# The recurrence of the odd layer: 32x32 chunk inverses by row substitution on VectorE in place of batched 128x128 products

## Chip, cores and metric

The kernel runs on one core of a Trainium2 chip. The metric is the device time of one execution in microseconds, lower is better. All data is float32.

## What is computed

The reference is a transformer of one block followed by a two-layer block (an even layer, an expert feed-forward, an odd layer, an expert feed-forward), for 512 tokens and 256 context tokens of width 1024. The change touches one part of the odd layer, a gated linear recurrence (RWKV-7) with 8 heads of 64, in both directions, which first runs over the context and then, from the state this leaves, over the tokens:

```python
def wkv7_step(S, inp):
    r, w, k, v, a, b = inp
    sa = jnp.einsum('bhvk,bhk->bhv', S, a)
    S = S * w[:, :, None, :] + sa[..., None] * b[:, :, None, :] + v[..., None] * k[:, :, None, :]
    return S, jnp.einsum('bhvk,bhk->bhv', S, r)

def direction(inp, d, S0):
    r, v, kk, w, a, k_eff, _ = inp
    a_d, k_d = a[:, :, d], k_eff[:, :, d]
    S, y = wkv7_scan(S0, r, w[:, :, d], k_d, v, -kk, kk * a_d, reverse=(d == 1))
    return S, y + jnp.sum(r * k_d * rk, -1, keepdims=True) * v
```

Computed by chunks of 32 tokens, each chunk of each head needs the inverse of I - N, where N is the strictly triangular 32x32 matrix of the products of the chunk's a and b vectors.

## The kernel before, in words

Every engine executes one list of instructions in the order in which the program emits them, and waits at semaphores. A `Core` object holds the counters and the PSUM banks of one line of work. `settle` makes an engine wait until all that the line has counted so far is done. `products` and `products_together` emit, group by group, the matmuls into a bank and the instruction that empties it; both begin with a settle of the engines they use, so that within a line one call waits for the one before it. `weave` takes generators and emits one piece of each in turn, up to the next `yield`; that order is the order on every engine.

The odd layer (`odd_layer`, L3132) loads its constants (`rwkv_constants`, L2901, with the loads at L140), projects the inputs (`rwkv_inputs`), runs the recurrence (`rwkv`, L2937), and goes on with neighbourhood attention and the output. The recurrence begins after all input is there, and the next stage begins with a load of X that waits for its end (L3164).

In `rwkv`, each direction d is one line with four PSUM banks, and `weave` alternates between the two lines. A line (`rwkv_direction`, L2696) goes through six rounds, one for each tile of 128 tokens: first the two context tiles, then the four token tiles. In this text the first two rounds are context rounds, and the other four (the code's `latent`) are token rounds. One round does this, for 8 heads, each with 4 chunks of 32 that stand on the diagonal of a 128x128 matrix:

- preparation: the decay and the rate from two small products (L2720, L2722), sums in the chunk (L2740), exponentials on ScalarE (L2746 to L2748), and element-wise products on VectorE (L2756 to L2774), which yield a, b, k and r with the decays multiplied in;
- transposes of a, b and k on TensorE (L402), with the banks emptied by VectorE and ScalarE in turn;
- `grams` (L2674, products at L2682, masks at L2689): b by a, a by b, and k by a, each masked to the chunks; b by a falls into blocks of 16 (B) and the part below them (Lo);
- the product of the masked k by a with the values (L2785), emptied at L2789, and Q = B + I (L2792);
- eleven jobs of `batched` (L2649): eight products of 128x128 by 128x128 each (L2655), emptied by ScalarE (L314) or, with an addition, by VectorE (L2664). They square B and accumulate the inverse of I - B in Q, and then solve in three more products with Lo between them;
- in token rounds two more grams with r;
- for each chunk three small products of 32 rows (L2830, L2832, L2834), emptied at L2841, and in token rounds one more product (L2816, L2839);
- four steps of the state, one for each chunk: product (L2854), addition (L2861), multiplication with the decay (L2862);
- in token rounds the output: products at L2871, L2875, L2878 and L2883, then three instructions of VectorE (L2892 to L2895).

## Time and profile before

| | |
|---|---|
| median of 3 runs | 4760.57 us (4752.04 to 4763.97) |
| profiled execution, span from first to last instruction | 4764.7 us |
| the recurrence (from L2713 to L2894) | 3096.7 to 3801.5 us, 704.8 us, 15% of the span |
| TensorE (PE) busy, whole span | 3841.3 us, 81% |
| VectorE (DVE) busy, whole span | 1379.7 us, 29% |
| ScalarE (ACT) busy, whole span | 724.6 us, 15% |

Of the profiled execution the span is what is listed; it lies 4.1 us above the median of the runs. In the rows below a matmul of float32 counts as two instructions, so a group of "x768" is 384 products of the code. "busy" of a group is the time in which at least one of its instructions ran; PE and PEld (the load of the stationary operand) overlap. PEclk 1.00 is the clock of 2.4 GHz, 0.50 that of 1.2 GHz. "<-" names what ended an engine's idle time. Busy share says little about the worth of a change here, since the stages have different limits; the reader should look at the stretch of the recurrence alone.

### The profile page before, as it was taken

Reading aid. Unit: us, or ns where it says so; the run is one execution under the profiler, and the core shown is the slowest. Engines: PE = TensorE matmul, PEld = TensorE weight load, DVE = VectorE, ACT = ScalarE, POOL = GpSimd, SP = SyncE. Lnnn points to the kernel's source line nnn. Section 1 sums busy time; section 2 is a strip of 40 time slices with the busy share of each in tenths; the row PEclk is TensorE's granted clock in tenths of the full one; section 3 lists DMA queues with packets and bytes.
Section 4 is the critical chain, followed back from the end, with each engine's and each line's share of the span. In section 5 each row is a group of like instructions: output and inputs, shape, how many; then the busy total and the mean of one; then the engine's idle time right before and its main releaser. Section 6 shows DMA issues by size and latency. Waiting matters only on the chain. (4 is left out here: it accounts for less than half of the span.)

```text
span 4764.7 us, 55924 instructions
## 1 busy us (share of the span) xinstructions
PE 3841.3 (81%) x23612; PEld 2364.9 (50%) x23612; DVE 1379.7 (29%) x2585; ACT 724.6 (15%) x1366; POOL 114.7 (2%) x88
## 2 busy tenths in 40 slices
PE   7998788888977875894899976877888769947776
PEld 3666356555523543783333324577777725632222
DVE  2312222322321077543100002245544423320000
ACT  1112001001011023311100001122222122210000
POOL 0000000000000000000011110000000000000000
PEclk9988798888888987996899998977888889969999
DMA  3200132443441100003799982000000011069999
GB/s 115 71 18 1 44 111 73 137 133 98 147 174 60 36 21 0 27 19 139 287 395 397 394 292 88 22 1 1 2 2 2 28 66 50 11 232 402 404 402 361
DMA packets 238285, 626.76 MB, mean 132 GB/s; under 512 B 38212, under 2 KB 90132, under 8 KB 230998
## 3 DMA queue, kind: packets, MB, share of 16 engines
q1 hardware_dynamic: 227990, 600.11, 33.6%
q0 software_dynamic: 10048, 23.07, 2.1%
q8 instruction: 190, 3.11, 0.3%
q14 instruction: 57, 0.47, 0.0%
HBM read 588.40 MB, written 34.75 MB: 131 GB/s over the span
## 5 line engine op out<-in xcount | busy, mean ns | idle before, releaser
L379 PE MATMUL bank<-weights_l,hT_l 128*128 128x512 f32 (+2 forms) x1824 | 605.7, 493 | 26.8 <-DMA weights_l<-in_w_in 20.0
L379 PEld LDWEIGHTS bank<-weights_l,hT_l 128*128 128x128 f32 x1824 | 386.2, 216 | 241.5 <-issue 173.6
L375 PE MATMUL bank<-hT_l,weights_l 128*128 128x512 f32 (+1 forms) x928 | 329.8, 518 | 39.6 <-DMA weights_l<-in_w_in 25.1
L1730 PE MATMUL bank<-expert_weights_l,expert_tokensT_l 128*32 128x512 f32 x3072 | 338.3, 596 | 11.4 <-DMA expert_weights_l<-in_moe_w 9.8
L1930 PE MATMUL bank<-expert_weights_l,expert_tokensT_l 128*64 128x512 f32 x1024 | 243.5, 622 | 82.8 <-DMA expert_weights_l<-in_moe_w 81.8
L375 PEld LDWEIGHTS bank<-hT_l,weights_l 128*128 128x128 f32 x928 | 179.2, 194 | 188.9 <-issue 165.3
L1240 PE MATMUL bank<-hT_l,gate_weights_r 128*128 128x512 f32 x384 | 213.7, 708 | 24.0 <-DMA gate_weights_r<-in_w_in 24.0
L1730 PEld LDWEIGHTS bank<-expert_weights_l,expert_tokensT_l 128*32 128x32 f32 x3072 | 107.8, 110 | 227.9 <-issue 226.9
L1930 PEld LDWEIGHTS bank<-expert_weights_l,expert_tokensT_l 128*64 128x64 f32 x1024 | 80.0, 142 | 236.2 <-issue 177.4
L1765 PE MATMUL bank<-expert_weights_l,rows 128*32 128x512 f32 x1536 | 167.9, 592 | 0.9 <-ACT rows L1805 0.9
L1930 PE MATMUL bank<-expert_weights_l,hiddenT_l 128*64 128x512 f32 x512 | 119.9, 610 | 47.0 <-DMA expert_weights_l<-in_moe_w 47.0
L1240 PEld LDWEIGHTS bank<-hT_l,gate_weights_r 128*128 128x128 f32 x384 | 83.5, 228 | 123.3 <-issue 104.5
L379 PE MATMUL bank<-weights_l,mixedT_l 128*128 128x256 f32 (+1 forms) x512 | 138.3, 433 | 2.4 <-ACT mixedT_l L314 1.4
L1486 PE MATMUL bank<-identity,normed_l 128*128 128x128 f32 x224 | 37.8, 351 | 126.7 <-ACT normed_l L452 75.3
L379 PEld LDWEIGHTS bank<-weights_l,mixedT_l 128*128 128x128 f32 x512 | 97.1, 190 | 42.8 <-issue 32.9
L1815 DVE TENSOR_TENSOR rows<-rows,bank 128x512 f32<-128x512 f32 x16 | 11.0, 688 | 368.5 <-ACT rows L1797 368.5
L1178 DVE SCALAR_TENSOR_TENSOR state_l<-state_l,exp_cumulative_l,bank 128x128 f32<-128x128 f32 x224 | 62.8, 343 | 176.5 <-PE bank L1161 173.8
L2664 DVE TENSOR_TENSOR rows<-rows,bank 128x512 f32<-128x512 f32 x96 | 65.9, 688 | 151.9 <-PE bank L2655 146.9
L1765 PEld LDWEIGHTS bank<-expert_weights_l,rows 128*32 128x32 f32 x1536 | 53.5, 110 | 111.7 <-issue 110.6
L1993 DVE TENSOR_TENSOR hidden_l<-silu_l,bank 128x512 f32<-128x512 f32 x16 | 11.0, 687 | 322.8 <-PE bank L1930 322.8
L2655 PE MATMUL bank<-rows,powers_then_steps_l 128*128 128x128 f32 x768 | 103.3, 294 | 0.0
L1613 POOL DMA_INDIRECT expert_rows_l<-normed_rows,row_numbers_l x16 | 15.4, 960 | 3651.6 <-DVE row_numbers_l L1609 3647.3
(471 smaller groups left out, 5247.8 us busy)
## 6 DMA issues: line engine op xcount, KB each, us to landing
expert_weights_l<-in_moe_w SPq DMA_DIRECT2D x192, 2048.0 KB, 24.9
ada_weights_r<-in_ada_w SPq DMA_DIRECT2D x48, 1024.0 KB, 5.0
weights_l<-in_w_in SPq DMA_DIRECT2D x10, 2048.0 KB, 8.0
weights_l<-in_w_in SPq DMA_DIRECT2D x16, 1024.0 KB, 5.3
gate_weights_r<-in_w_in SPq DMA_DIRECT2D x12, 1024.0 KB, 6.4
weights_l<-in_od_w_in SPq DMA_DIRECT2D x7, 1024.0 KB, 5.4
gate<-gate_rows_r SPq DMA_DIRECT2D x24, 256.0 KB, 2.4
weights_l<-in_ev_w_in SPq DMA_DIRECT2D x3, 2048.0 KB, 10.6
```

What stands on the lines that cost most here:

```text
L375: ins = pe.matmul(bank[:n, :m], w_sb[:, k, s:s + n], xT[:, k, t:t + m], start=k == 0, stop=k == kt - 1)
L379: ins = pe.matmul(bank[:rows_of_tile(x), :n], x, w_sb[:, k, :n], start=k == 0, stop=k == kt - 1)
L1178: ins = dve.scalar_tensor_tensor(out=new[:, s], in0=old[:, s], scalar=cum[:, hh, c * CH + edge:c * CH + edge + 1], in1=kv_bank[i % 2][:, s ...
L1240: ins = pe.matmul(bank[:, :], w[:, k, s:s + P], hT[:, k, :], start=k == 0, stop=k == KT - 1)
L1486: ins = pe.transpose(bank[:, (t - a) * P:(t - a) * P + P], xn[:, t, k * P:k * P + P], ident[:, :])
L1613: pool.indirect_dma_start(out=rows[:, q, :], out_offset=None, in_=normed[w], in_offset=bass.IndirectOffsetOnAxis(ap=idx[:, q:q + 1], axis= ...
L1730: return pe.matmul(bank[q * STRIP:(q + 1) * STRIP, :], xs[:, k, e, g * STRIP:(g + 1) * STRIP], w[:, j, h * HALF:(h + 1) * HALF], start=k = ...
L1765: return pe.matmul(bank[q * STRIP:(q + 1) * STRIP, :], rows, w2[:, f % DEEP, m * HALF:(m + 1) * HALF], start=f == first, stop=f == last)
L1815: dve.tensor_tensor(hid, hid, w3_bank[:, :], ALU.mult)
L1930: ins = pe.matmul(bank[h * S:h * S + S, :], rows(k), ring[r][:, k % DEEP, h * HALF:(h + 1) * HALF], start=k == 0, stop=k == KT - 1)
L2655: ins = pe.matmul(bank[:, j * P:j * P + P], lhs[:, m, :], rhs[:, m, :], start=True, stop=True)
L2664: return e.tensor_tensor(dst[:, s, :], add[:, s, :], src, ALU.add)
```

## The change

The inverse of each 32x32 matrix is computed directly. The masked 128x128 products b by a and a by b become 32x32 products of the chunks alone (64 matrices of both directions). They are stored to DRAM and loaded again, so that each of 64 partitions holds one 32x32 matrix; VectorE then substitutes row by row, with two instructions for each of 30 rows, and the inverses go back through DRAM: for direction 0 into the diagonal blocks of Q, for direction 1 into a tile whose blocks VectorE transposes into Q. Ten of the eleven `batched` jobs, the masks 2 and 3, Lo, Am, A2 and the addition of I fall away.

The preparation of both directions becomes a third line, `ahead`, which works one round ahead of the two others; the substitution is cut into six pieces that are emitted between the pieces of the current round. The banks are dealt 3, 3 and 2 instead of 4 and 4. The tiles that preparation writes exist twice. The transposes and the product with the values are emptied by ScalarE. In the steps of the state, the products with b and k are accumulated in the same bank as the product with the state, so that one instruction of VectorE is left for each step; the output is accumulated in one bank along with the steps, and the bonus term is written to Y by the preparation. In `rwkv_constants` the four loads into `sums_in_chunk` go, the mask load becomes two smaller ones, and one small constant is added.

```diff
+    out["above_diagonal"] = np.tile(np.triu(np.ones((32, 32), f), 1), (4, 1))
-def rwkv_direction(core, d, C, U, kkT, vnat, ups, cols, consts, mats, Y):
+ROUNDS = (((4, 5, 0, 1, 2, 3), (5, 4, 3, 2, 1, 0)))
+def rwkv_prepare(core, rnd, C, U, kkT, ups, cols, consts, sides, Y):
+    products(core, 4, fill, take, lambda i: "v" if i < 2 else "s", ready=True)
+    core.settle(act)
+    for side in sides:
+        act.activation(side.L[:, :, :], side.L[:, :, :], ACT.Sigmoid).then_inc(step.sem, step.one())
+    yield True
...
+    products(core, 4, fill, take, lambda i: "s")
+    yield True
+    for d, side in enumerate(sides):
+        dve.wait_ge(core.emptied_s.sem, decayed + 2 * d + 2)
+        dve.scalar_tensor_tensor(out=side.L[:, :, :], in0=b_[:, :, :], scalar=-1.0, in1=bc(cols[:, COL_KA, :], P),
+                                 op0=ALU.add, op1=ALU.mult).then_inc(step.sem, step.one())
+        dve.scalar_tensor_tensor(out=a_[:, :, :], in0=kk, scalar=-1.0, in1=a_[:, :, :],
+                                 op0=ALU.mult, op1=ALU.mult).then_inc(step.sem, step.one())
+        dve.wait_ge(step.sem, step.n - 1)
+        dve.tensor_tensor(b_[:, :, :], b_[:, :, :], kk, ALU.mult).then_inc(step.sem, step.one())
+        dve.wait_ge(step.sem, step.n)
+        dve.tensor_tensor(b_[:, :, :], b_[:, :, :], k_[:, :, :], ALU.mult).then_inc(step.sem, step.one())
+    yield True
+    def fill(pe, d, banks):
+        lhs, rhs = (two[d][1], two[d][0]) if d == 0 else (two[d][0], two[d][1])
+        for j in range(RCT):
+            for c in range(NCH):
+                s = slice(c * CH, c * CH + CH)
+                for odd, bank in enumerate(banks):
+                    r = slice(odd * RN, odd * RN + RN)
+                    ins = pe.matmul(bank[s, j * CH:j * CH + CH], lhs[r, j, s], rhs[r, j, s], start=True, stop=True)
+        return ins
+    def take(e, d, odd, bank):
+        return e.tensor_tensor(sides[d].M[:, odd * RCT:odd * RCT + RCT, :],
+                               bank[:, 0:RCT * CH].rearrange("p (m n) -> p m n", n=CH), mid(upper, RCT), ALU.mult)
+    dve.wait_ge(sent.sem, sent.n)
+    products_together(core, [2, 2], fill, take)
+    made = core.emptied_v.sem, core.emptied_v.n
+    yield made
...
+def chunk_inverses(core, rnd, sides, made, sent, q, product, scratch, signals):
+    nc = core.nc
+    sp, dve = nc.sync, nc.vector
+    landed, stepped, inverted, returned = signals
+    matrices, inverses = scratch
+    blocks = [dram(matrices, d * RH * NCH * CH * CH, [[CH, P], [NCH * CH * CH, RH], [1, CH]]) for d in range(2)]
+    sp.wait_ge(*made)
+    for side, block in zip(sides, blocks):
+        sp.dma_start(block, side.M[:, :, :]).then_inc(sent.sem, sent.sixteen())
+    sp.wait_ge(sent.sem, sent.n)
+    sp.dma_start(q[:, :, :], matrices.rearrange("b (i j) -> b i j", j=CH)).then_inc(landed.sem, landed.sixteen())
+    yield True
+    dve.wait_ge(landed.sem, landed.n)
+    part = [list(x) for x in q[:, :, :].ap][0]
+    base, at = q[:, :, :], q[:, :, :].offset
+    linked(dve, stepped, dve.memset(bass.AP(base.tensor, at, [part, [CH + 1, CH]]), 1.0))
+    for j in range(1, CH - 1):
+        n = CH - 1 - j
+        left = bass.AP(base.tensor, at + j, [part, [CH, j], [0, n]])
+        row = bass.AP(base.tensor, at + j * CH + j + 1, [part, [0, j], [1, n]])
+        out = q[:, 0:j, j + 1:CH]
+        here = product[:, 0:j * n].rearrange("p (a b) -> p a b", b=n)
+        linked(dve, stepped, dve.tensor_tensor(here, left, row, ALU.mult))
+        ins = dve.tensor_tensor(out, out, here, ALU.add)
+        if j < CH - 2:
+            linked(dve, stepped, ins)
+            if j % 5 == 0:
+                yield True
+    ins.then_inc(inverted.sem, inverted.one())
+    sp.wait_ge(inverted.sem, inverted.n)
+    sp.dma_start(inverses.rearrange("b (i j) -> b i j", j=CH), q[:, :, :]).then_inc(returned.sem, returned.sixteen())
+def load_inverses(core, rnd, sides, scratch, returned):
+    sp = core.nc.sync
+    inverses = scratch[1]
+    sp.wait_ge(returned.sem, returned.n)
+    for d, side in enumerate(sides):
+        if rnd:
+            past(sp, [side.inverse_used[rnd - 1]])
+        arrived = side.inverse_landed
+        if d:
+            sp.dma_start(side.turned[:, :, :], dram(inverses, RH * NCH * CH * CH, [[CH, P], [NCH * CH * CH, RH], [1, CH]])) \
+                .then_inc(arrived.sem, arrived.sixteen())
+            continue
+        for c in range(NCH):
+            s = slice(c * CH, c * CH + CH)
+            sp.dma_start(side.Q[s, :, s], dram(inverses, c * CH * CH, [[CH, CH], [NCH * CH * CH, RH], [1, CH]])) \
+                .then_inc(arrived.sem, arrived.sixteen())
+def rwkv_round(core, side, rnd, C, vnat, consts, Y):
...
+    transposes(core, [(R_a, [a_[:, c, :] for c in range(RCT)]), (bn[:, :], [b_[:, c, :] for c in range(RCT)]),
+                      (kn[:, :], [k2_[:, c, :] for c in range(RCT)])], C["ident"], lambda i: "s")
+    yield True
+    grams(core, [(k2_, a_, [(N2, mk(1))])])
...
+    arrived = side.inverse_landed
+    if d:
+        core.settle(dve)
+        dve.wait_ge(arrived.sem, 16 * (rnd + 1))
+        for c in range(NCH):
+            s = slice(c * CH, c * CH + CH)
+            dve.transpose(Q[s, :, s], side.turned[s, :, :]).then_inc(step.sem, step.one())
+    else:
+        pe.wait_ge(arrived.sem, 16 * NCH * (rnd + 1))
+    batched(core, [(B, Q, R, None)])
+    side.inverse_used.append((filled.sem, filled.n))
+    if latent:
+        grams(core, [(b_, r2_, [(N2, mk(0))]), (k2_, r2_, [(R, mk(0))])])
...
+    products_together(core, [2, 2, 1] if latent else [2, 2], fill, take)
...
+    def stepped(i):
+        if i:
+            pe.wait_ge(emptied.sem, v0 + i)
+        for h, (e, m, p) in enumerate(at):
+            o = slice(p * RN, p * RN + RN)
+            ins = pe.matmul(s_bank[i % 2][e:e + RN, o], phi[e:e + RN, i, o], S[e:e + RN, i, p, :],
+                            start=False, stop=True, skip_group_check=True)
+        ins.then_inc(filled.sem, filled.one())
+        dve.wait_ge(filled.sem, f0 + i + 1)
+        cc = i if d == 0 else NCH - 1 - i
+        dve.tensor_tensor(S[:, (i + 1) % NCH], s_bank[i % 2][:, 0:RCT * RN].rearrange("p (c n) -> p c n", n=RN),
+                          bc(edge[:, cc], RN), ALU.mult).then_inc(emptied.sem, emptied.one())
...
+    added(0)
+    stepped(0)
+    if latent:
+        within()
+    added(1)
+    yield True
+    for i in range(1, NCH):
+        if latent:
+            carried(i - 1)
+        stepped(i)
+        if i + 1 < NCH:
+            added(i + 1)
...
+        y = Y[:, :, tt * P:tt * P + P]
+        dve.tensor_tensor(y, y, y_bank[:, :].rearrange("p (c n) -> p c n", n=P), ALU.add) \
+            .then_inc(emptied.sem, emptied.one())
...
-    masks = sb("masks", [P, 2, 4, P])
-    tri = sb("sums_in_chunk", [P, 2, 2, P])
-    one_pair = sb("identity_and_zero", [P, 2, RCT, RN])
+    masks = sb("masks", [P, 2, 2, P])
+    upper = sb("above_diagonal", [P, CH])
+    one = sb("identities", [P, RCT, RN])
-        for kind in range(2):
-            core.load(tri[:, d, kind, :], I["tri"][d, 2 * kind])
-    core.load(masks[:, :, :, :], I["masks_f"].rearrange("d k s t -> s d k t"))
+        core.load(masks[:, d, :, :], I["masks_f"][d, 0:2].rearrange("k s t -> s k t"))
+    core.load(upper[:, :], I["above_diagonal"])
...
+        q = sb("chunks_by_partition", [2 * RH * NCH, CH, CH])
+        product = sb("row_products", [2 * RH * NCH, CH * CH // 4])
+        with core.beside(3) as beside:
+            ahead.begin(beside.bank[3:5])
+            beside.bank = beside.bank[0:3]
+            for side, line in zip(sides, (core, beside)):
+                line.settle(dve)
+                dve.memset(side.S[:, 0], 0.0).then_inc(line.step.sem, line.step.one())
+                dve.memset(side.Q, 0.0).then_inc(line.step.sem, line.step.one())
+                line.settle(sp)
+            def prepared(rnd):
+                for made in rwkv_prepare(ahead, rnd, C, U, kkT, consts[0], col, consts_, sides, Ys):
+                    if made is not True:
+                        yield from chunk_inverses(ahead, rnd, sides, made, sent, q, product, scratch,
+                                       (landed, stepped, inverted, returned))
+                    yield True
+            weave(prepared(0))
+            load_inverses(ahead, 0, sides, scratch, returned)
+            for rnd in range(len(ROUNDS[0])):
+                weave(*([prepared(rnd + 1)] if rnd + 1 < len(ROUNDS[0]) else []),
+                      *(rwkv_round(line, side, rnd, C, vnat, consts_, Ys[side.d])
+                        for side, line in zip(sides, (core, beside))))
+                if rnd + 1 < len(ROUNDS[0]):
+                    load_inverses(ahead, rnd + 1, sides, scratch, returned)
+            for eng in (sp, pe, dve, act):
+                ahead.settle(eng)
+                eng.wait_ge(returned.sem, returned.n)
```

## Rows read from the trace of the kernel before

**Rows 1.** Page: the span, and the busy time of three engines (share, instructions).

```profile
span 4764.7 us, 55924 instructions
...
PE 3841.3 (81%) x23612; PEld 2364.9 (50%) x23612; DVE 1379.7 (29%) x2585; ACT 724.6 (15%) x1366; POOL 114.7 (2%) x88
```

**Rows 2.** Busy time by stretch: the recurrence, then one context round and one token round.

```profile
core 0: us, PE busy (x) PEld busy (x) DVE busy (x) ACT busy (x) POOL busy (x), PEclk, DMA share, GB/s
3096.70:3801.50 704.80, 572.39 (x7576) 536.59 (x7576) 350.18 (x584) 160.73 (x287) 0.00 (x0) 0.82 0.01 2
...
3203.90:3309.80 105.90, 84.55 (x1071) 80.64 (x1070) 49.89 (x85) 26.96 (x48) 0.00 (x0) 0.81 0.01 2
...
3432.75:3555.50 122.75, 100.95 (x1363) 94.10 (x1362) 62.65 (x106) 26.96 (x48) 0.00 (x0) 0.83 0.01 2
```

**Rows 3.** The same view, the phases of that token round; columns as in rows 2.

```profile
3432.75:3454.00 21.25, 10.97 (x62) 9.67 (x61) 13.33 (x24) 9.64 (x19) 0.00 (x0) 0.75 0.00 0
3454.00:3468.50 14.50, 10.54 (x118) 9.76 (x118) 12.09 (x20) 0.60 (x1) 0.00 (x0) 0.85 0.01 1
3468.50:3475.50 7.00, 7.00 (x35) 7.00 (x35) 3.60 (x4) 0.12 (x1) 0.00 (x0) 0.50 0.01 2
3475.50:3514.30 38.80, 38.80 (x340) 38.80 (x340) 11.23 (x17) 15.64 (x27) 0.00 (x0) 0.97 0.00 1
3514.30:3531.40 17.10, 12.28 (x485) 10.87 (x484) 11.19 (x19) 0.96 (x2) 0.00 (x0) 0.92 0.02 4
3531.40:3544.00 12.60, 9.87 (x142) 8.96 (x144) 7.10 (x18) 0.00 (x0) 0.00 (x0) 0.50 0.01 2
3544.00:3555.50 11.50, 11.50 (x193) 9.04 (x190) 4.11 (x7) 0.00 (x0) 0.00 (x0) 0.92 0.01 3
```

**Rows 4.** Groups of instructions in the recurrence: busy us, mean ns of one, idle before.

```profile
L2655 PE MATMUL bank<-rows,powers_then_steps_l 128*128 128x128 f32 x768 | 103.3, 294 | 0.0
L2664 DVE TENSOR_TENSOR rows<-rows,bank 128x512 f32<-128x512 f32 x96 | 65.9, 688 | 151.9 <-PE bank L2655 146.9
...
L2883 PE MATMUL bank<-decay_or_r_l,states_l 64*64 64x32 f32 x512 | 16.4, 220 | 0.0
...
L2682 PE MATMUL bank<-decay_before_or_a_l,rate_or_b_l 64*128 64x128 f32 x192 | 15.9, 311 | 0.0
...
L2682 PE MATMUL bank<-rate_or_b_l,decay_before_or_a_l 64*128 64x128 f32 x192 | 13.4, 280 | 0.0
...
L2682 PE MATMUL bank<-decay_or_r_l,rate_or_b_l 64*128 64x128 f32 x128 | 8.9, 278 | 0.0
```

**Rows 5.** VectorE in order of time: start us, duration us; pairs where one waits for the other.

```profile
1453.31 0.18 DVE L1469 TENSOR_SCALAR norm_scales<-mod_columns 128x16 f32<-128x16 f32 x1 [0.27 <-ACT mod_columns L314]
1453.52 0.18 DVE L1470 TENSOR_TENSOR norm_scales<-norm_scales,norm_gains_l 128x16 f32<-128x16 f32 x1
...
3410.14 0.42 DVE L2861 TENSOR_TENSOR states_l<-bank,powers_then_steps_l 128x256 f32<-128x256 f32 x1 [1.32 <-PE bank L2854]
3410.59 0.42 DVE L2862 TENSOR_TENSOR states_l<-states_l,chunk_decay_l 128x256 f32<-128x256 f32 x1
```

**Rows 6.** The chain that ended last, near 4232 us: start us, us; a store, then a load.

```profile
4231.57 1.33 DMA selection<-gates_l
4232.96 2.39 DMA numbers_l<-selection
```

**Rows 7.** DMA issues of the page: count, KB each, median us from issue to landing.

```profile
expert_weights_l<-in_moe_w SPq DMA_DIRECT2D x192, 2048.0 KB, 24.9
...
gate<-gate_rows_r SPq DMA_DIRECT2D x24, 256.0 KB, 2.4
...
bias_l<-in_na_bias SPq DMA_DIRECT2D x8, 384.0 KB, 3.5
```

**Rows 8.** SyncE's queue while it issues the odd layer's constants: start us, us.

```profile
2852.39 4.28 SPq L140 DMA_DIRECT2D sums_in_chunk_l<-in_tri  x2
...
2858.45 1.87 SPq L140 DMA_DIRECT2D sums_in_chunk_l<-in_tri  x2
```

More of the change, by code:

```diff
@@ L2707, in rwkv_direction, with fill @@
-    sc = slice(d * LORA, d * LORA + LORA)
+    masks, upper, _, sent = consts
+    latent = rnd >= NC
+    two = [side.two[rnd % 2] for side in sides]
+    def fill(pe, i, bank):
+        d = i % 2
+        sc, cs = slice(d * LORA, d * LORA + LORA), sides[d].span(rnd)
+        if i < 2:
+            return pe.matmul(bank[:, :], U[sc, LT_W, cs], w2[sc, :], start=True, stop=True)
+        for c in range(RCT):
+            ins = pe.matmul(bank[:, c * P:c * P + P], a2[sc, c * P:c * P + P], U[sc, LT_A, cs], start=True, stop=True)
+        return ins
@@ new lines, in rwkv_prepare, with fill, take @@
+    core.settle(act)
+    for side in sides:
+        act.activation(side.L[:, :, :], side.L[:, :, :], ACT.Sigmoid).then_inc(step.sem, step.one())
+    yield True
+    def fill(pe, i, bank):
+        d, kind = i // 2, 1 - i % 2
+        for c in range(RCT):
+            ins = pe.matmul(bank[:, c * P:c * P + P], sides[d].L[:, c, :], masks[:, d, kind, :], start=True, stop=True)
+        return ins
+    def take(e, i, bank):
+        d, kind = i // 2, 1 - i % 2
+        a_, _, k_, r_, _ = two[d]
+        src = bank[:, :].rearrange("p (c n) -> p c n", n=P)
+        if kind:
+            return e.activation(a_[:, :, :], src, ACT.Exp, scale=-RHO)
+        e.activation(k_[:, :, :], src, ACT.Exp, scale=RHO)
+        return e.activation(r_[:, :, :], src, ACT.Exp, scale=-RHO)
```

365 lines of the change are left out of this document (162 added, 203 removed).

## The prediction, made before the changed kernel was run

> **What bounds the kernel now.** I read the page first: over the whole span TensorE is busy for 81% and VectorE for 29% [rows 1]. That is a mean over stages with different limits, so I read the recurrence by itself: it lasts 704.8 us, of which TensorE is busy 572.4, VectorE 350.2 and ScalarE 160.7 [rows 2]. The recurrence begins when all its input is there and the next stage waits for its end, so what it loses or gains is passed on in full. Within it a token round takes 122.75 us and a context round 105.9 [rows 2]; the rest is the start.
>
> The phases of a token round show who sets the pace [rows 3]. In order: preparation and the first transposes (21.25 us, TensorE half idle); the rest of the transposes and the grams (14.5); the product with the values (7.0, at a granted clock of 0.50); the batched products (38.8, TensorE busy without a gap); grams with r and chunk products (17.1); state steps (12.6); output and the start of the next preparation (11.5). So a third of a round is the batched products, and they are bound by TensorE: VectorE waits 146.9 us for them in all [rows 4].
>
> **What is removed.** A round has 22 batched jobs (11 for each line) in 38.8 us, 1.76 us each; two remain. That takes 20 x 1.76 = 35.3 us of TensorE out of each round, all on the path. Two of three grams go: (15.9 + 13.4) / 6 = 4.9 us of TensorE a round [rows 4], with twelve masks of VectorE. VectorE also loses the batched additions (65.9 / 6 = 11.0 us a round [rows 4]), Q = B + I, one of two instructions of each state step, and four evictions a round that ScalarE takes over; ScalarE loses more than it gains.
>
> **What is added.** The substitution has 30 rows with two instructions each; row j works on j x (31 - j) elements, 4960 in the sum, 9920 for both. Where one small instruction waits for the one before it, starts lie 0.21 us apart at 16 elements and 0.45 us at 256 [rows 5]: 0.194 us each plus 1.0 ns an element. So 60 x 0.194 + 9.9 = 21.6 us of VectorE a round, for both directions together. The second instruction at 256 elements reads a broadcast operand, and lasts no longer for it (0.42 us both). The small products of chunks are 64 a round; the nearest row has 64x64 by 32 columns, 16.4 us for 256 products or 0.064 us each [rows 4]: 4.1 us of TensorE. Their masks are four of 128 elements (0.3 us each, 1.2). The four 32x32 transposes of VectorE are in no row; from below 0.21 us each, from above 0.69 (a full 512), I take 0.45 for 256 elements: 1.8 us.
>
> Nine DMAs a round go through SyncE's queue, which has nothing else here: two stores of 1024 pieces of 128 bytes, a load of 256 KB, a store of 256 KB, and five loads. Piece by piece the nearest rows are a store that took 1.33 us and a load of 1024 pieces of 4 bytes that took 2.39 [rows 6]: 3.8 us from below. By bytes, 256 KB landed in 2.4 us and 384 KB in 3.5 [rows 7], with issue on top. I take 9 us for stores and load together and 3 for the store back; the top end is two legs of 24.9 us, the slowest landing of the page [rows 7]. VectorE waits for this load at the head of the first piece of substitution, and behind it in VectorE's queue stand the evictions of the chunk products, for which both lines wait. In a token round the batched products, two grams and their masks (about 13 us) lie between issue and wait and cover it; in a context round half of that.
>
> **The new round.** Per token round TensorE keeps 100.95 - 35.3 - 4.9 + 4.1 = 65 us, and VectorE about 57: 62.65, less 31 (11.0 additions, 7.3 masks, 2.4 Q + I, 4.1 evictions, 3 of the steps, the rest small), plus 25. I lay the new order of pieces out in four stretches.
> (a) Preparation, transposes, one gram, product with the values. TensorE has 10.97 + 10.54 + 7.0 - 4.9 = 23.6 us [rows 3, 4], with three lines to fill its gaps; the others have less. 24 us, where it was 42.75.
> (b) Small products, batched solve, grams with r, first piece of substitution. TensorE 4.1 + 3.5 + 4.4 (a gram with r is 8.9 / 4, twice [rows 4]) = 12; VectorE 1.2 + 1.8 + 4.9 + 2.9 = 10.8. Three and two banks do not let them overlap much: 22 us.
> (c) Chunk products, state steps, output, beside four pieces of substitution. TensorE 12.28 - 4.4 + 9.87 + 11.5, less 2.2 for the bonus product = 27 us [rows 3]; VectorE 16.4 + 4.7 + 3.4 = 24.5. Each step's single VectorE instruction queues behind a piece of some 4 us, while TensorE has both lines' products of about 5 us: 33 us.
> (d) Last piece, Y, the rest of preparation (ten instructions) and the bonus: VectorE alone, 12 us; the lines have run out of pieces.
> Sum 91 us. A context round is 17 us shorter, as before [rows 2]: 74, and 76 where it prepares a token round. Before the first round stands a preparation that nothing covers: 18 for products, exponentials and element-wise work (the phase of 21.25 us [rows 3], less its first transposes), 5.5 for the small products and masks, 9 for the DMAs, 22 for the substitution, 3 back: 57.5 us. The last round has nothing to prepare: its old phases after preparation are 101.5 us, less 35.3, and less some 10 for grams and masks, plus 6 for its transposes: 62. The recurrence is 57.5 + 74 + 76 + 3 x 91 + 62 = 542.5 us: 162 less. The constants' four loads were 6.15 us on SyncE's queue [rows 8], and the preparation of the layer waits for that queue; with a mask load and a small constant in their place I take 3 us off. Together 165: span 4764.7 - 165 = 4599.7, and 4.1 us lower against the median of the runs, 4596 us.
>
> **Rivals.**
> 1. The cover fails (0.23). Each hand-over between lines waits for VectorE behind a piece, and nothing overlaps. A token round is then 122.75 - 35.3 - 7.3 - 2.4 - 2.5 = 75, plus 21.6 + 9 + 4.1 + 1.2 + 1.8 = 113; a context round 96: 644 us, a gain of 61 and 4697 us in all. With half the cover lost it is 4650. For it: in-order queues, fewer banks. Against: VectorE has 60 us idle in a token round [rows 2].
> 2. The cover is nearly perfect (0.15). Each round takes what its busier engine takes, 65 or 49 us: 57.5 + 2 x 49 + 3 x 65 + 62 = 412 and 4466 us; halfway 4530. For it: the product with the values ran at 0.50 after gaps [rows 3] which a third line may close.
> 3. The clock falls (0.06). TensorE will be busy for 65 of 91 us instead of 101 of 123, and its steps, where it was busy 9.87 of 12.6 us, already ran at 0.50, which is 1.2 GHz [rows 3]. If all does, the phases granted 0.75 to 0.92 need 78 us for 45: on the path some 25 us more a token round and 15 a context round, 130 in all: 4726 us. The Trainium skill, "TensorE: Matmul & The Clock Gate", Part 1, speaks against the change here: the slow clock is the default and only activity lifts it. By that rule this rival would be the forecast; the trace bears it out in the steps, but not in the phase before them (0.92 at 12.28 of 17.1 us).
> 4. Slower than before (0.03): VectorE's wait for the load. If a leg takes the 24.9 us of the page's slowest landing, two legs are 50 us, of which the cover takes 10: 41 more in each of five rounds and before the first, and the way back adds 14 a round and 22 at the start: 340 us, 4936 in all. It decides from 165 / 6 = 27 us a round. Against: that row is 2 MB on busy engines; the DMA share is 0.01 here [rows 2]. The Trainium skill, "DMA: Bandwidth & Descriptors", under Specifications, asks for at least 512 bytes a transfer for full rate, with read-modify-write below; no row here prices pieces of 128 bytes.
> The remaining 0.53 is the forecast's, with 4550 to 4640 us as its own range.
>
> **How the numbers follow.** The forecast gives 4596. The range reaches into rivals 1 and 2, to 4530 and 4680; what it leaves out is the better end of rival 2, the worse of 1, and 3 and 4, some 0.2. About 0.3% (14 us) is what a measurement tells from no change. Only mixtures of rivals 3 and 4 lie there: same 0.03. Slower is rival 4 with 0.03 and another 0.01 of such mixtures: 0.04. The rest is faster, 0.93.
>
> **What would show it.** Right: no batched jobs but the solve; TensorE busy some 350 us in a recurrence of about 540; substitution instructions at 0.2 to 0.45 us a start, 21 to 22 us a round; DMA waits of VectorE only in context rounds; four phases of 24, 22, 33 and 12 us. Wrong: pieces of substitution with TensorE idle beside them in (c) (rival 1); a recurrence under 500 us (2); a clock of 0.50 in (a) (3); VectorE idle for tens of us before the memset of the diagonal (4).

## The result, and the profile after

The changed kernel takes 4639.33 us (median of 4 runs, 4638.57 to 4640.86) beside 4759.74 us for the kernel before: a ratio of 0.9748, 95% interval 0.9736 to 0.9761. That is 120 us less, where 165 had been forecast; the forecast's time was 4596 us. Its profiled execution has a span of 4636.4 us. On the page, TensorE lost 177 us of busy time against [rows 1] and VectorE 59:

```profile
span 4636.4 us, 52147 instructions
...
PE 3664.5 (79%) x22076; PEld 2176.7 (47%) x22076; DVE 1320.7 (28%) x2714; ACT 656.3 (14%) x1258; POOL 114.5 (2%) x88
```

Busy time by stretch: the recurrence, the preparation that nothing covers, two context rounds, three token rounds that prepare a next one, and the last round. They answer to [rows 2].

```profile
core 0: us, PE busy (x) PEld busy (x) DVE busy (x) ACT busy (x) POOL busy (x), PEclk, DMA share, GB/s
3084.10:3672.60 588.50, 405.06 (x6040) 357.44 (x6036) 291.86 (x713) 92.91 (x179) 0.00 (x0) 0.67 0.06 12
3084.10:3136.90 52.80, 13.83 (x184) 10.27 (x180) 31.51 (x84) 7.86 (x17) 0.00 (x0) 0.56 0.07 15
3136.90:3209.50 72.60, 54.06 (x812) 49.30 (x812) 39.49 (x106) 15.62 (x30) 0.00 (x0) 0.64 0.08 16
3209.50:3290.80 81.30, 58.80 (x816) 51.91 (x816) 44.84 (x114) 15.62 (x30) 0.00 (x0) 0.63 0.09 18
3290.80:3396.60 105.80, 76.22 (x1105) 66.52 (x1104) 52.66 (x126) 15.62 (x30) 0.00 (x0) 0.66 0.06 11
3396.60:3502.10 105.50, 74.89 (x1105) 65.16 (x1104) 52.57 (x125) 15.62 (x30) 0.00 (x0) 0.68 0.06 11
3502.10:3605.00 102.90, 69.66 (x1107) 61.20 (x1107) 52.42 (x125) 15.62 (x30) 0.00 (x0) 0.71 0.06 12
3605.00:3672.60 67.60, 57.61 (x916) 53.09 (x915) 18.37 (x36) 6.94 (x12) 0.00 (x0) 0.73 0.01 2
```

The recurrence fell from 704.8 to 588.5 us, 116.3 less, which accounts for the result. The column to watch is PEclk, the last but two: the granted clock of the recurrence fell too, from 0.82 to 0.67. Behind the recurrence nothing changed (963.8 us, before 963.2). It begins 12.6 us earlier in this trace than in that of before. That isn't the change: the run below that has the kernel before up to the recurrence (`e2_before_one_batched`, constants and all) also began it at 3081.9 us, and the traces of all the other runs begin it between 3080 and 3088 us. It is a difference between executions, and the trace of before is the odd one.

The same view, the second of the three token rounds cut at the prediction's stretches (a) to (d), which answer to [rows 3]:

```profile
3396.60:3419.10 22.50, 14.70 (x137) 13.48 (x136) 8.72 (x14) 13.23 (x26) 0.00 (x0) 1.00 0.00 1
3419.10:3448.70 29.60, 18.55 (x256) 16.60 (x256) 10.15 (x27) 2.39 (x4) 0.00 (x0) 0.52 0.09 19
3448.70:3485.40 36.70, 35.27 (x694) 32.56 (x696) 22.09 (x60) 0.00 (x0) 0.00 (x0) 0.65 0.01 2
3485.40:3502.10 16.70, 6.37 (x24) 2.52 (x21) 11.61 (x27) 0.00 (x0) 0.00 (x0) 0.59 0.17 31
```

(a) is at full clock and shorter than its forecast. (b) is at 0.52; TensorE waits in it for 11 us. (c) has TensorE busy for 35.27 of 36.70 us and VectorE for 22.09, so by this row TensorE is its bound, not VectorE. In (d) TensorE is busy for 6.37 of 16.70 us. TensorE in order of time inside (b): start us, busy us, and in brackets the idle time before.

```profile
3419.14 0.76 PE L2817 MATMUL bank<-decay_before_or_a_l,rate_or_b_l 64*32 64x32 f32 x64 [2.19 <-DVE rate_or_b_l L2807]
3420.67 0.88 PE L2817 MATMUL bank<-rate_or_b_l,decay_before_or_a_l 64*32 64x32 f32 x64 [0.78 <-DVE chunk_matrix_l L2821]
3421.74 3.75 PE L2656 MATMUL bank<-rows 128*128 128x128 f32 x16 [0.19 <-issue]
3426.49 2.08 PE L2683 MATMUL bank<-decay_or_r_l,rate_or_b_l 64*128 64x128 f32 x16 [0.99 <-ACT rows L314]
...
3434.74 3.79 PE L2656 MATMUL bank<-rows 128*128 128x128 f32 x16 [3.12 <-DVE rows L2957]
3439.52 2.08 PE L2683 MATMUL bank<-decay_or_r_l,rate_or_b_l 64*128 64x128 f32 x16 [0.99 <-ACT rows L314]
```

A batched job had been priced at 1.76 us; it takes 3.75 and 3.79. A gram with r takes 2.08 where the prediction had 1.1 (4.4 for four).

The groups of the recurrence: busy us, mean ns of one, idle time before.

```profile
L3006 PE MATMUL bank<-rows,b_rows_l 32*64 32x64 f32 x768 | 69.4, 277 | 0.0
L3007 PE MATMUL bank<-values_l,k_rows_l 32*64 32x64 f32 x768 | 67.1, 268 | 0.0
...
L2888 DVE TENSOR_TENSOR chunks_by_partition_l<-chunks_by_partition_l,row_products_l 64x30 f32<-64x30 f32 (+9 forms) x180 | 58.1, 323 | 6.2
L2887 DVE TENSOR_TENSOR row_products_l<-chunks_by_partition_l 64x30 f32<-64x30 f32 (+9 forms) x180 | 58.0, 322 | 5.3
...
L3015 PE MATMUL bank<-states_l,steps_l 64*64 64x64 f32 x768 | 45.6, 285 | 0.0
...
L2957 DVE STREAM_TRANSPOSE rows<-chunk_inverse_l 32x256 f32<-32x256 f32 x24 | 10.4, 433 | 0.6
```

L3006 and L3007 are the products of b and k that the change adds straight into the bank of the steps; by busy time they are now TensorE's costliest groups (what that number is worth comes up below). And VectorE's wait for the chunks to come back from memory (us in total, times, longest):

```profile
DVE chunks_by_partition_l L2880 <- DMA chunks_by_partition_l<-chunk_matrices: 16.6, 3, 6.5
```

### The profile page after: what moved, and what is told of

It reads as the page before. It is cut to its first block and busy times, and to the rows that moved or that the text cites. A ratio compares the mean times of both kernels' runs of the same rounds, so it can differ in the third digit from the quotient of the medians.

```text
span 4636.4 us, 52147 instructions
## 1 busy us (share of the span) xinstructions
PE 3664.5 (79%) x22076; PEld 2176.7 (47%) x22076; DVE 1320.7 (28%) x2714; ACT 656.3 (14%) x1258; POOL 114.5 (2%) x88
## 5 line engine op out<-in xcount | busy, mean ns | idle before, releaser
L1731 PE MATMUL bank<-expert_weights_l,expert_tokensT_l 128*32 128x512 f32 x3072 | 338.4, 596 | 11.7 <-DMA expert_weights_l<-in_moe_w 10.0
L1816 DVE TENSOR_TENSOR rows<-rows,bank 128x512 f32<-128x512 f32 x16 | 11.0, 687 | 368.9 <-ACT rows L1798 368.9
L2307 PE MATMUL bank<-identity,scores_l 128*128 128x128 f32 (+1 forms) x704 | 98.5, 282 | 5.6 <-ACT scores_l L2293 5.6
L2307 PEld LDWEIGHTS bank<-identity,scores_l 128*128 128x128 f32 (+1 forms) x704 | 91.1, 191 | 19.1 <-ACT scores_l L2293 9.8
```

The source lines that it names most:

```text
L1731: return pe.matmul(bank[q * STRIP:(q + 1) * STRIP, :], xs[:, k, e, g * STRIP:(g + 1) * STRIP], w[:, j, h * HALF:(h + 1) * HALF], start=k = ...
L1816: dve.tensor_tensor(hid, hid, w3_bank[:, :], ALU.mult)
L2307: ins = pe.matmul(t_bank[m % 2][:b - a, i * P:i * P + P], s[:, n % R, a:b], core.ident[:, :], start=True, stop=True)
```

## The experiments

State of the theory before them: the recurrence is 46 us over its forecast since TensorE's small products run at 1.2 GHz in (b), (c) and (d), and since (d) is longer than thought. The rival is that VectorE's pieces stand on the path, and TensorE is only cold because it waits for them. "Cold" stands here for the level of 1.2 GHz.

Beside the experiments the kernel before had medians from 4752.7 to 4759.7 us, so a difference of less than some 7 us between two experiments can't be told from none. Each difference in us below is from the changed kernel's 4639.33 unless another is named.

**The substitution alone.** In `chunk_inverses`, only the row j = 1 is worked out; the 29 other rows are left out, so what arrives are not the inverses:

```
     for j in range(1, CH - 1):
+        if j > 1:
+            if j % 5 == 0:
+                yield True
+            continue
```

> The changed kernel with the substitution cut to its first row (rows 2 to 30 of 30 are left out, so the inverses that arrive are not inverses); its DMAs, waits and the places of its pieces stay. VectorE loses some 20.5 us of work a round, and the same in the prologue. Theory (rounds are set by TensorE, whose small products run at the 1.2 GHz level for much of a round; VectorE's pieces lie beside them): the prologue gives its 20.5 us, the five rounds that prepare at most 5 us each, so about 4600 us (4590 to 4620), and the token rounds stay over 98 us. Rival (the pieces stand on the path, and the cold clock only follows from TensorE waiting for them): each round gives 12 to 18 us, the granted clock of the recurrence rises from 0.67 towards 0.8, and the time is 4520 to 4560 us.

4575.41 us (ratio 0.9629, 0.9604 to 0.9653), 64 less than the changed kernel. The stretches, the whole recurrence and then the same token round:

```profile
3083.90:3606.60 522.70, 385.68 (x6040) 340.43 (x6036) 180.78 (x365) 92.89 (x179) 0.00 (x0) 0.71 0.07 14
...
3352.25:3447.80 95.55, 69.69 (x1105) 60.65 (x1104) 34.17 (x68) 15.62 (x30) 0.00 (x0) 0.73 0.06 13
```

The first preparation gave 21.0 us (52.8 to 31.8), the three token rounds 10.6, 10.0 and 11.7, the context rounds 4.8 and 7.8, the last nothing. Neither expectation held: a token round gives back about half of its 21 us of substitution. The two traces show by which way. TensorE's wait ahead of the second group of chunk products (L2979) goes from 3.68 to 1.45 us, and the stretch behind the last step from 16.2 to 13.3: 5 us are waits for VectorE. Another 5.4 us go in between, from that second group to the last step (3449.39 to 3485.87 us, then 3403.36 to 3434.47), where TensorE is idle for 0.74 us in either run; there the clock rises from 0.65 to 0.79. With all but one row gone a token round still takes 95.55 us, 4.5 over what the forecast gave it with substitution, at a clock of 0.73. So most of the cold clock doesn't come from these pieces.

**The removal alone**, in the kernel before: ten of the eleven `batched` jobs are left out, with their `yield`s, and nothing is put in their place, so Q is not the inverse here either. The last call stays.

```
-        batched(core, [(N2, Am, B, None), (A2, B, Am, None)])
-        yield True
...
-        batched(core, [(R, Lo, B, R)])
-        yield True
         batched(core, [(B, Q, R, None)])
```

> The kernel before with one of its eleven batched products a round and line (the other ten, with their evictions, are left out, so the inverse is not one); nothing is added. It measures the removal by itself, in the place of the term of 35.3 us a round. By the prediction's step it gives 212 us less: about 4548 us, recurrence 493 us, at an unchanged clock. Theory (what is left is small products that don't hold TensorE's clock, so part of the removed time comes back as cold small products without anything added): 130 to 180 us less, 4580 to 4630 us, with the granted clock of the recurrence at 0.65 to 0.75 in place of 0.82.

4534.57 us (0.9542, 0.9518 to 0.9566), 221 less than before:

```profile
3081.90:3564.00 482.10, 348.50 (x5656) 311.85 (x5656) 283.72 (x488) 74.82 (x143) 0.00 (x0) 0.77 0.01 2
```

The prediction's 212 was right to within 9 us, on the better side. The theory that part of it comes back as cold products without anything added had 130 to 180 us and a clock of 0.65 to 0.75; it is refuted (221 us, 0.77). What was mis-priced is what the change adds, and the order in which it puts it: of 221 us it gives back 100.

**The cover alone.** The next preparation is issued wholly ahead of the round in every queue, in place of between its pieces:

```
-                weave(*([prepared(rnd + 1)] if rnd + 1 < len(ROUNDS[0]) else []),
-                      *(rwkv_round(
+                if rnd + 1 < len(ROUNDS[0]):
+                    weave(prepared(rnd + 1))
+                weave(*(rwkv_round(
```

> The changed kernel with each next round's preparation, substitution included, wholly ahead of the round in every queue, in place of woven between its pieces: the price of the cover. From stretches of the changed kernel: six preparations of 53 to 57 us, and rounds as long as the last one, which has no preparation beside it (67.6 us with tokens, some 45 us for the two of the context): about 330 + 360 = 690 us of recurrence against 588, so 4740 us (4720 to 4770). If TensorE is the bound of the woven rounds through its clock, the cover is poor, and this costs less than 80 us (under 4720); if the weaving hides nearly all of VectorE's preparation, it costs over 150 us (over 4790).

4756.34 us (1.0003, 0.9991 to 1.0015): the weaving is worth 117 us, all of the change's gain. A token round falls apart into the preparation and the round itself:

```profile
3334.70:3396.00 61.30, 15.60 (x193) 12.47 (x194) 34.89 (x89) 9.83 (x20) 0.00 (x0) 0.57 0.06 13
3396.00:3464.30 68.30, 59.04 (x913) 52.90 (x911) 18.45 (x36) 5.92 (x11) 0.00 (x0) 0.69 0.03 6
```

That is 129.6 us against 105.5: the weaving hides 24 of the 61.3 us of preparation, and 37 it does not. The time lies in the middle case of the expectation (4720 to 4770 us): less than half of the preparation is covered, but that is more than the case of a poor cover (under 4720 us) would have it.

**The leftover preparation early.** What `rwkv_prepare` yields behind the chunk matrices (keys, receptances, bonus) is issued with the first two pieces of substitution (arguments are cut to `...`):

```
-                for made in rwkv_prepare(...):
-                    if made is not True:
-                        yield from chunk_inverses(...)
-                    yield True
+                made = rwkv_prepare(...)
+                for _ in range(3):
+                    next(made)
+                    yield True
+                inverses = chunk_inverses(..., next(made), ...)
+                next(inverses)
+                next(made)
+                yield True
+                next(made)
+                next(inverses)
+                yield True
+                next(inverses)
+                next(made, 0)
+                yield True
+                for _ in inverses:
+                    yield True
```

> The changed kernel with one edit of order: what the preparation has left after the chunk matrices (keys, receptances and the bonus of both directions) is issued with the first two pieces of the substitution instead of behind its last one, so that nothing but the last pieces stands at the end of the round. Theory (the last stretch of a token round, 16.7 us, is VectorE's leftover preparation behind the last step, with TensorE waiting for it and at 0.59 of its clock): 6 to 10 us less in each of the three token rounds that prepare, 2 to 5 in the two of the context, so 4605 to 4620 us. Rival (VectorE has the same sum to do and each piece then comes later, the steps' states wait behind it): within 5 us of 4639, or slower.

4599.07 us (0.9677, 0.9656 to 0.9698), 40 less and below the 4605 to 4620 that were expected:

```profile
3370.55:3466.00 95.45, 73.09 (x1104) 64.02 (x1104) 52.33 (x126) 15.63 (x30) 0.00 (x0) 0.70 0.06 13
```

A token round is as short with the substitution in this order as it was without it in the other (95.55). That is no proof that the substitution costs nothing in this order, since no run has both edits. In the changed kernel ten instructions of VectorE of 0.68 or 0.69 us (3489.2 to 3496.1 us, in (d)) come behind the last piece, when both lines are out of work. Issued early they save 10 us a token round, the upper end of what was expected, and 13 us in the context round that prepares a token round (81.3 to 67.9), which was not.

**Finer pieces**: `weave(preparation, left, preparation, right)`, three rows a piece in place of five, and the leftover preparation early here too, between the DMAs of the chunk matrices and the first piece of rows. So the run to compare with is the one before (4599 us).

> The changed kernel with the preparation at double pace: a piece of it after each line's piece in place of after both, the substitution in pieces of three rows, and the leftover preparation between the DMA's issue and the first piece of rows. Finer pieces at the same sum of work. Theory (what the order of the pieces costs is the late end of the preparation; the last stretch goes as in the kernel with the leftover issued early, and shorter pieces hold up the steps' states less): token rounds at 90 to 95 us in place of 105, 4580 to 4600 us. Rival (VectorE's pieces now come between the two lines' own work, in the masks of the grams and the states): token rounds over 97 us, 4605 us or more.

4619.9 us (0.9716, 0.9695 to 0.9737), 21 more than with the coarse pieces. Against the changed kernel the context rounds gained (66.8 and 72.4 us where they were 72.6 and 81.3) and so did the first token round (100.2 for 105.8); the two later ones took 105.6 each. The rival held (token rounds over 97 us), and the coarse pieces stayed.

**The added products in turns of two chunks.** In `added`, for each head and a pair of chunks, with one wait for both banks:

```
+            for kind in range(2):
+                for j in (i, i + 1):
+                    r, bank = rows(j), s_bank[j % 2]
+                    if kind == 0:
+                        pe.matmul(bank[e:e + RN, o], bn[r, n], B[r, m, RN:], start=h < 2, stop=False, skip_group_check=True)
+                    else:
+                        pe.matmul(bank[e:e + RN, o], kn[r, n], vnat[r, tt, n], start=False, stop=False,
+                                  skip_group_check=True)
```

> The changed kernel with the products of b and k into the steps' bank issued for two chunks in turn (two row groups and two banks alternate) in place of chunk by chunk; the products are the same, only their order changes, and those of a pair of chunks wait for both banks. Theory (these products cost 58 ns each at the 2.4 GHz level and some 120 at 1.2 GHz because neighbours share rows of the array; in the kernel before, four chunks in turn took some 25 ns a product): 128 products a round and line pair, each 25 to 60 ns less, 3 to 7 us a round, 20 to 40 us in all: 4600 to 4620 us. Rival (the rows shared are not what sets them, or the added wait for both banks gives it back): within 6 us of 4639, with the mean start-to-start time of these products unchanged.

4605.49 us (0.9679, 0.9661 to 0.9696), 34 less, within the 4600 to 4620 that were expected. The two groups:

```profile
L3009 PE MATMUL bank<-rows,b_rows_l 32*64 32x64 f32 x768 | 35.6, 274 | 10.9 <-DVE states_l L3025 10.9
L3011 PE MATMUL bank<-values_l,k_rows_l 32*64 32x64 f32 x768 | 34.2, 264 | 0.0
```

Their busy time has halved, while one of them lasts as long as before (274 ns for 277): twice as many are in flight. But neighbours had stopped sharing two things, their rows and the place to which they add. So a further run keeps the rows and parts only the places: all heads of b, then all of k.

> The changed kernel with the products of b and k into the steps' bank in another order within a chunk: first all heads of b, then all of k, in place of b and k of one head in turn. Neighbours then never add into the same place and alternate between the two halves of the array's columns, but still share their 32 rows and their bank. It tells what halved these products in turns of two chunks. Theory (neighbours that share rows of the array run one after the other): 58 ns a product stays, busy time of the two groups 130 to 137 us together, 4633 to 4646 us. Rival (what they wait for is the place to which the product before adds): some 30 ns a product, 70 us together, and about 4605 us as in turns of two chunks.

4632.17 us (0.9745, 0.9732 to 0.9759), no difference from the changed kernel (0.9748) that can be told. The time is the theory's, but the busy times that went with it misled: 43.0 and 39.8 us, 83 together, where the theory had 130 to 137 and the rival 70. In the changed kernel b and k alternate and each group's busy time covers the other's. Starts tell it. The changed kernel, one chunk (16 products) from its first start to where the next group starts:

```profile
3470.69 0.34 PE L3006 MATMUL bank<-rows,b_rows_l 32*64 32x64 f32 x4
...
3471.82 0.66 PE L3036 MATMUL bank<-decay_or_r_l,states_l 64*64 64x32 f32 x16
```

The run with b before k, one chunk:

```profile
3467.15 0.68 PE L3006 MATMUL bank<-rows,b_rows_l 32*64 32x64 f32 x16
3467.66 0.63 PE L3009 MATMUL bank<-values_l,k_rows_l 32*64 32x64 f32 x16
3468.22 0.66 PE L3038 MATMUL bank<-decay_or_r_l,states_l 64*64 64x32 f32 x16
```

That makes 1.13 us and 1.07 us for 16 products, 71 and 67 ns each (the 58 ns of the expectation leave out the passage to the next group). In turns of two chunks, at the same clock, 32 products take from 3458.16 to 3459.30 us, 36 ns each. So parting the places of the sums alone saves next to nothing, and parting rows and banks halves the time. Whether the row group or the bank does it, these runs leave open, since the two chunks differ in both.

**Holding the clock.** Products of 128x128 by 128x512 that nobody reads, in idle times of TensorE: 2 ahead of the chunk matrices, 2 ahead of the second line's product with the inverse, 9 ahead of the bonus's product. The helper, without its calls:

```
+def spare(core, w, n):
+    pe = core.nc.tensor
+    nb, g0 = len(core.bank), len(core.emptied_by)
+    if g0 >= nb:
+        pe.wait_ge(*core.emptied_by[g0 - nb])
+    for _ in range(n):
+        pe.matmul(core.bank[g0 % nb][:, :], core.ident[:, :], w, start=True, stop=True)
```

> The changed kernel with products of 128x128 by 128x512 added on TensorE that nobody reads, in three of its idle times of each round: 2 ahead of the chunk matrices, 2 ahead of the second line's product with the inverse, 9 ahead of the bonus's product. One takes about 0.9 us at the 2.4 GHz level and 1.8 at 1.2. Theory (the cold clock is what the idle times bring, and it costs the small products behind them): the granted clock of the token rounds rises from 0.68 to over 0.8 and they take 92 to 98 us in place of 105, so 4600 to 4625 us although 13 products are added to a round. Rival (the small products lose the clock by themselves, idle or not): clock within 0.04, time 4639 to 4665 us, the added products being paid in full where they outlast the idle time.

4606.49 us (0.9689, 0.9668 to 0.971), 33 less for work that was added. The token round, then TensorE in order of time in it (L2703 is the spare group; the clock of (b) is read from L2656 and L2683):

```profile
3390.70:3486.05 95.35, 74.31 (x1132) 58.90 (x1130) 52.41 (x126) 15.63 (x30) 0.00 (x0) 0.89 0.06 13
```

```profile
3417.31 2.02 PE L2656 MATMUL bank<-rows 128*128 128x128 f32 x16 [0.17 <-issue]
3420.32 1.16 PE L2683 MATMUL bank<-decay_or_r_l,rate_or_b_l 64*128 64x128 f32 x16 [0.99 <-ACT rows L314]
...
3423.55 1.98 PE L2703 MATMUL bank<-decay_base_l,identity 128*128 128x512 f32 x4
3426.74 2.05 PE L2656 MATMUL bank<-rows 128*128 128x128 f32 x16 [1.21 <-DVE rows L2969]
```

The batched job is back at 2.02 us from 3.75, the gram at 1.16 from 2.08. The clock of the round rose from 0.68 to 0.89 and the round lost 10 us, with the order and the work of the rest unchanged: cold products were a cost of their own. To see which of the three places matters, the next run keeps only the 9 at the end:

> The changed kernel with only the 9 spare products ahead of the bonus's product, at the end of a round's preparation; the 4 others of that experiment are gone. It tells where the warm clock is worth something. Theory: the stretch that follows, the start of the next round, is at full clock already in the changed kernel, and the cold ones (second line's product with the inverse, steps) come 20 us later behind another idle time, so 9 spare products at the end give little: 4630 to 4645 us. Rival (a clock held at the end lasts into those stretches): 4605 to 4620 us, as with all 13.

4634.1 us (0.9741, 0.9726 to 0.9756). As the theory had it, the 9 at the end are worth about nothing by themselves. The four others were not run alone, so whether they bring all of the 33 us, or only beside the 9, is not shown.

**All together.** The leftover early and turns of two chunks:

> The kernel with the leftover preparation issued early (4599 us) and, besides, the products of b and k in turns of two chunks, as in the run before the last. If both hold and don't share a stretch, 3 to 6 us a round less than 4599: 4565 to 4585 us. If TensorE's stretch of steps waits for VectorE's pieces now, under 10 us less: 4590 to 4600.

4576.67 us (0.9619, 0.9603 to 0.9635), in the first of its two ranges. With 2, 2 and 4 spare products at the places where this order leaves TensorE idle (the third is now ahead of the first line's products for the steps), and then with 3, 4 and 6:

> The kernel with leftover preparation issued early and products in turns of two chunks (4577 us), with spare products of 128x512 in the three idle times that it leaves TensorE: 2 ahead of the chunk matrices, 2 ahead of the second line's product with the inverse, 4 ahead of the first line's products for the steps (there TensorE waits 7 us for the eviction of the steps). If cold small products still set these rounds, the granted clock of the token rounds goes from 0.73 to 0.83 or more and they take 86 to 89 us in place of 92: 4550 to 4565 us. Rival (with the other two edits VectorE sets the rounds, TensorE being idle at its full clock for much of the last 20 us of a round): within 6 us of 4577, whatever the clock.

> The same as the run with all three edits but with 3, 4 and 6 spare products in the three places in place of 2, 2 and 4. Longer fillings hold the clock more surely but outlast the idle time: a product too many costs 0.9 us where the clock is full and 1.8 where it isn't. If the clock was still falling in the leaner run, this one is 3 to 10 us faster than it; if not, up to 10 us slower.

4552.23 us (0.9576, 0.956 to 0.9591), and with more of them 4556.82 (0.9573 to 0.9605), the same. A token round without the spare products (4577 us):

```profile
3362.20:3454.20 92.00, 63.46 (x1104) 55.37 (x1104) 52.05 (x126) 15.62 (x30) 0.00 (x0) 0.74 0.07 13
```

With them (4552 us), the whole recurrence and then a token round:

```profile
3085.60:3585.40 499.80, 360.31 (x6124) 297.47 (x6120) 290.23 (x713) 92.96 (x179) 0.00 (x0) 0.80 0.07 14
...
3360.30:3448.10 87.80, 67.21 (x1120) 55.67 (x1120) 52.24 (x127) 15.63 (x30) 0.00 (x0) 0.85 0.07 14
```

This version leaves nothing out and is faster than both kernels: 87 us under the changed one and 4.2% under the one before. The three edits, alone worth 40, 34 and 33 us, give 87 of their sum of 107 together. The intervals of the three overlap; by the recurrence alone, in one trace each, they are 43, 33 and 34 us, and 89 together.

## Why the prediction was right, and where its terms were off

The forecast mechanism held: the removed products are off the path, the substitution is partly hidden, and the net is a gain. The stated range held the time. That the forecast's own narrower range held it too, by 0.7 us (4639.3 against its edge of 4640), is luck: the gain is 45 us short of the 165 forecast. The recurrence was to take 542.5 us and took 588.5, and one of the prediction's signs of being right failed with it: TensorE was to be busy for some 350 us in it and was for 405. By the prediction's own steps:

- **Removal**, 35.3 us a round or 212 in all: 221 by itself. Right, and 9 us too low.
- **Substitution**, 21.6 us of VectorE: from the memset at 3112.53 to 3133.98 us in the first preparation, 21.45. The line through two pairs of rows [rows 5] priced 60 instructions to 1%.
- **Small products**, 4.1 us: 0.76 to 0.88 us for 32, so 1.7 for 64. Too dear; the row taken was of products of 64x64 by 32 columns, these are 32x32. **Masks** 287 ns (0.3), **transposes** 433 ns (0.45): right.
- **DMAs**, 9 us for the trip: 6.5 us from the last mask at 3106.0 to the memset, the wait of the row above. It stands three times (6.5, 5.2 and 4.9 us), before the first round and in the two context rounds, and never in a token round, as forecast. Rival 4 is refuted: two stores in pieces of 128 bytes took 1.0 to 2.0 us to issue, and VectorE's wait for the load is 6.5 us at most. The Trainium skill, "DMA: Bandwidth & Descriptors", Specifications, gives 512 bytes as the least transfer for full rate, with read-modify-write below it. No run here has larger pieces to compare, so what the small ones cost is not shown; with them the whole trip took the 6.5 us.
- **Preparation that nothing covers**, 57.5: 52.8, by the small products (2.4 us too dear) and the DMAs (2.5 too dear).
- **Context rounds**, 74 and 76: 72.6 and 81.3. **Last round**, 62: 67.6.
- **Token rounds**, 91: 105.8, 105.5 and 102.9, together 41 of the 46 us. Here the prediction failed, in three terms. (a), 24 us: 22.5. **(b), 22 us: 29.6**: two batched solves at 3.8 in place of 1.76 and four grams at 2.08 in place of 1.1 make 8.0 us more, the small products 2.4 less. The step took these durations from phases at 0.97 and 0.92 of the clock [rows 3] and put them where TensorE comes out of waits. **(c), 33: 36.7**: the step took TensorE's old phases over as they were, 27 us. The changed kernel issues the products of b and k chunk by chunk, where the one before had four chunks in turn, and it is cold for much of the stretch (0.65). TensorE was busy for 35.3 us, so it was the bound for most of it, and not VectorE's pieces as the prediction argued; the run with one row was 5.4 us shorter there all the same, by a higher clock and not by a shorter wait. **(d), 12: 16.7**: VectorE's own work in it is 11.6 us, as priced; what was left out are its waits, 2.3 and 0.9 us for the bonus's products, at 1.2 GHz again, and 1.4 for the first product of the next preparation.
- **Constants**, 3 us off: not shown. With the old constants the kernel before without its batched jobs began its recurrence at 3081.9 us, the changed one at 3084.1.

Rival 3 had a chance of 0.06 and the mechanism of most of the error. It did not come in full: its sign, a clock of 0.50 in (a), failed (1.00), and the mean over the recurrence was 0.67. In (b) and (d), where TensorE waits for 11 of 29.6 and 10 of 16.7 us, the clock was 0.52 and 0.59, and idle time filled with work nobody reads raised that of a token round to 0.89 and gave 33 us. By the Trainium skill, "TensorE: Matmul & The Clock Gate", Part 1, the slow clock is the default and activity lifts it. The rows of (b) and (d) and the run with spare products agree. The prediction had set the rule aside on the strength of one phase at 0.92 [rows 3]. In (c) the trace is not plainly on its side: there the clock was 0.65 with TensorE busy for 35.27 of 36.70 us. The prediction should have priced the small and late products at both levels: by (b) alone 8 us a token round. Rival 1's sign, TensorE idle beside the pieces in (c), did not come (1.4 of 36.7 us). Its price for a kernel without any cover was 644 us of recurrence, 101 above the forecast, and the unwoven run needed 705, so the cover was worth more (117 us) and the parts cost more than the prediction said.

## What to carry to other kernels

When a long dense stretch of TensorE is replaced by small products around another engine's work, price what is left at both clock levels, in particular what comes after each wait. Lay out by hand which work comes last in a woven round: ten small instructions behind the last piece cost 10 us a token round, and moving them took the most off the recurrence of the single edits (43 us for 33 and 34). Where an engine is idle anyway and the work behind it runs cold, work that nobody reads can pay: 33 us here. The place decides: 9 such products where the next work was already at the full clock gave nothing.

## What the runs showed of the hardware

First, the granted clock can fall without any idle time of TensorE. In the same token round of the changed kernel, two neighbouring stretches of steps in which TensorE has no gap:

```profile
3464.00:3475.00 11.00, 11.00 (x299) 10.35 (x298) 6.56 (x17) 0.00 (x0) 0.00 (x0) 0.97 0.01 3
3475.00:3485.40 10.40, 10.40 (x192) 9.93 (x192) 7.36 (x22) 0.00 (x0) 0.00 (x0) 0.53 0.01 2
```

The first is at 2.4 GHz and the second at 1.2; before the fall the engine had run nothing but small float32 products of 32 to 64 rows and of 128 rows by 64 to 128 columns. Such products alone do not always bring the fall: in the run with one row of substitution the same products, without a gap too, were at 1.00 from 3417.0 to 3434.4 us. What decides between the two, no run shows.

Second, the busy time of a group can mislead where two groups alternate: 69.4 and 67.1 us of L3006 and L3007 are largely the same time, and only starts gave the cost of one product (71 ns at 2.4 GHz, and 36 with neighbours in other rows and another bank).
